# Narrow products among dense blocks, a second z block moved behind the Gram products, and fill products in four waits of TensorE

## What is computed

```python
h = rms_norm(x, pre_mix_norm)
p_r, p_k, p_v, p_c, z_rwkv, z_conv = split(h @ w_in)
# RWKV-7, per head, token after token
def step(S, inp):
    r_t, w_t, k_t, v_t, a_t, b_t = inp
    sa = einsum('bhvk,bhk->bhv', S, a_t)
    S = S * w_t + sa * b_t + v_t * k_t
    return S, einsum('bhvk,bhk->bhv', S, r_t)
# convolution branch: 31 causal taps per channel, then layer norm and silu
c = silu(layer_norm(conv31(u * sigmoid(gate)) + dw_b))
merged = sigmoid(z_rwkv) * (y @ w_rwkv_out) + sigmoid(z_conv) * (c @ w_conv_out)
x = x + rms_norm(merged @ w_out)
x = x + rms_norm((silu(h @ w_gate) * (h @ w_up)) @ w_down)   # h = rms_norm(x, ...)
```

## Time and profile before

| | |
|---|---|
| runs, three | median 1368.31 us, 1367.41 to 1369.19 |
| the profiled execution | 1369.3 us, its span 1367.6 us |
| busy: TensorE | 1321.0 us, 97% of the span |
| busy: VectorE, ScalarE, GpSimd | 995.3, 774.4, 115.8 us |
| mean granted clock of TensorE | 0.988 |
| chain of work that ended last | TensorE 89%, VectorE 7%, issue 2%, ScalarE 2%, DMA 1% |

### The profile page before, as it was taken

The page is one execution under the profiler, slowest core; times in us unless marked ns, Lnnn a source line. Parts: engine busy times, 40 slices in busy tenths (PEclk is TensorE's granted clock), DMA queues, the critical chain, the costliest instruction groups (busy, mean ns, idle before and its releaser), DMA issues.

```text
span 1367.6 us, 30059 instructions
## 1 busy us (share of the span) xinstructions
PE 1321.0 (97%) x12384; PEld 1260.9 (92%) x12384; DVE 995.3 (73%) x1636; ACT 774.4 (57%) x1353; POOL 115.8 (8%) x151
## 2 busy tenths in 40 slices
PE   7999999999999999999997999999999998999998
PEld 6998979889989999989996899999999888999986
DVE  5769998969876665585898867887565666887754
ACT  5596775559455444464669755444455465644443
POOL 3000000000002110000103002221000100122100
PEclk9999999989999999999999999999999999999999
DMA  7634611222545555545572354556563621555561
GB/s 242 205 122 148 194 64 34 86 72 94 193 147 185 182 186 175 187 142 181 177 227 84 103 183 161 182 185 199 173 196 133 224 93 63 185 185 184 176 210 61
DMA packets 197811, 212.70 MB, mean 156 GB/s; under 512 B 8973, under 2 KB 186925, under 8 KB 197565
## 3 DMA queue, kind: packets, MB, share of 16 engines
q1 hardware_dynamic: 195132, 201.46, 45.9%
q0 software_dynamic: 2464, 9.52, 2.4%
q10 hardware_dynamic: 96, 0.02, 0.0%
HBM read 209.33 MB, written 1.65 MB: 154 GB/s over the span
## 4 chain that ended last, share of the span: by engine, by line
PE 89%; DVE 7%; issue 2%; ACT 2%; DMA 1%; SPq 0%; DVEq 0%; ACTq 0%
PE pb L473 21%; PE pb L475 21%; PE pb L474 21%; PE pb L2428 2%; PE pb L2762 1%; PE pb L2763 1%; PE pb L2764 1%; DVE pj L1690 1%; PE pb L2253 1%; PE pb L2264 1%; DVE w_lo L517 1%; PE pb L2697 1%; PE pb L2372 1%; PE pb L2373 1%; PE pb L2374 1%
## 5 line engine op out<-in xcount | busy, mean ns | idle before, releaser
L517 DVE TENSOR_TENSOR w_lo<-raw,w_hi 128x1024 fp32r<-128x1024 f32 (+2 forms) x384 | 466.1, 1217 | 137.6 <-ACT w_hi L511 136.8
L511 ACT ACTIVATE w_hi<-raw 128x1024 fp32r<-128x1024 f32 (+2 forms) x384 | 396.5, 1041 | 280.9 <-PE pb L475 219.5
L473 PE MATMUL pb<-x_hi,w_hi 128*128 128x256 f32 x1848 | 526.0, 285 | 3.1 <-DVE w_lo L517 2.8
L474 PE MATMUL pb<-x_lo,w_hi 128*128 128x256 f32 x1848 | 523.1, 283 | 0.0
L475 PE MATMUL pb<-x_hi,w_lo 128*128 128x256 f32 x1848 | 523.1, 283 | 0.0
L473 PEld LDWEIGHTS pb<-x_hi,w_hi 128*128 128x128 f32 x1848 | 355.0, 192 | 6.0 <-DVE w_lo L517 3.9
L474 PEld LDWEIGHTS pb<-x_lo,w_hi 128*128 128x128 f32 x1848 | 355.0, 192 | 0.2
L475 PEld LDWEIGHTS pb<-x_hi,w_lo 128*128 128x128 f32 x1848 | 354.9, 192 | 0.0
L766 POOL TENSOR_TENSOR sub<-sub,rstd 128x256 f32<-128x256 f32 x66 | 71.8, 1102 | 568.9 <-ACT sub L1159 568.9
L473 PE MATMUL pb<-act_hi,w_hi 128*128 128x256 f32 x392 | 110.9, 283 | 0.0
L475 PE MATMUL pb<-act_hi,w_lo 128*128 128x256 f32 x392 | 110.9, 283 | 0.0
(11 more groups left out here) (369 smaller groups left out, 2273.3 us busy)
## 6 DMA issues: line engine op xcount, KB each, us to landing
raw<-in_ffn_w_up_dram SPq DMA_DIRECT2D x55, 1024.0 KB, 5.1
raw<-in_w_in_dram SPq DMA_DIRECT2D x28, 1024.0 KB, 5.2
raw<-in_ssd_w_in_dram SPq DMA_DIRECT2D x20, 1024.0 KB, 5.3
raw<-in_ffn_w_down_dram SPq DMA_DIRECT2D x16, 1024.0 KB, 5.0
raw<-in_fox_w_in_dram SPq DMA_DIRECT2D x16, 1024.0 KB, 5.8
raw<-in_ffn_w_down_dram SPq DMA_DIRECT2D x16, 896.0 KB, 5.0
raw<-in_ffn_w_gate_dram SPq DMA_DIRECT2D x11, 1024.0 KB, 5.2
raw<-in_ssd_w_out_dram SPq DMA_DIRECT2D x8, 1024.0 KB, 5.9
```

The source lines that it names most:

```text
L473: pe.matmul(o, w_hi[m][:, k, :], hi[:, k0 + k, :], start=first and k == 0, stop=False)
L474: pe.matmul(o, w_hi[m][:, k, :], lo[:, k0 + k, :], start=False, stop=False)
L511: act.activation(piece(ly, u, w_hi[m], nk, m), raw_piece(ly, u, s, nk, m), ACT.Copy).then_inc(sem("w_hi_ready"), 1)
L517: dve.tensor_tensor(piece(ly, u, w_lo[m], nk, m), raw_piece(ly, u, s, nk, m), piece(ly, u, w_hi[m], nk, m).bitcast(F32), ALU.subtract).the ...
```

## The change

The code of the change does five things.

1. **Start.** Eight products of a 128x128 fp32 matrix with itself (`keep_busy`; nothing reads the result) are written behind the first transposes, ahead of layer rk.
2. **Triangle.** The second part of the triangle products is no longer a run behind block 3 of ug: eight of its products follow each k step inside the block, through a new hook `between`. The first part stays where it was.
3. **Inverse and z.** The first z block is taken out of chunk 0 and stands ahead of the chunks, with eight of the second group's 64 inverse products behind each of its k steps. In chunks 0 to 3, which hold two z blocks, the second goes behind the Gram products (`Z_FRONT`). Its evacuation on VectorE moves behind the mask and one tap, ahead of the state sum; its `w_hi` on ACT moves behind `v_rows`. The wait for z evacuations is split: the x products wait for all the blocks before them, the state products for the front ones.
4. **Chunk 4.** Seven fill products ahead of the wait for the copies of u, that is ahead of the state products.
5. **Squares.** Ten fill products behind each of the two `post_squares`, ahead of up0 and ssd_z.

Hunk 473 is in `pe_layer`, 1048 on ScalarE, 1728 on VectorE, those from 2264 on TensorE:

```diff
+        FIRST_SINGLE = Z_CHUNK.index(1)
+        Z_FRONT = [1 if n == 2 else n for n in Z_CHUNK]
...
@@ -473,6 +476,11 @@
                         mm = pe.matmul(o, w_lo[m][:, k, :], hi[:, k0 + k, :], start=False, stop=final and k == nk - 1)
+                        if between and k < nk - 1:
+                            between(u, m, k)
                     mm.then_inc(sem("block_done"), 1)
+                    if between:
+                        between(u, m, nk - 1)
...
@@ -1048,8 +1059,7 @@
-                for j in range(BANKS + Z_FIRST[c], min(BANKS + Z_FIRST[c + 1], len(L["z"]) * M_PER_UNIT)):
-                    z_head(j)
+                z_heads(Z_FIRST[c], Z_FIRST[c] + Z_FRONT[c])
...
                 if c + 1 < NCHUNK:
                     v_rows(c + 1)
+                z_heads(Z_FIRST[c] + Z_FRONT[c], Z_FIRST[c + 1])
...
@@ -1728,7 +1739,7 @@
-                    if i < Z_CHUNK[c]:
+                    if i < Z_FRONT[c]:
                         z_evac(Z_FIRST[c] + i, Z_FIRST[c] + i + 1)
...
                     mask_products(c + 1)
+                taps = DVE_EARLY + sum(DVE_TAPS[:c])
+                if Z_FRONT[c] < Z_CHUNK[c]:
+                    conv_taps(taps, taps + 1)
+                    taps += 1
+                    z_evac(Z_FIRST[c] + Z_FRONT[c], Z_FIRST[c + 1])
+                if c + 1 < NCHUNK:
                     state_sum(c)
-                conv_taps(DVE_EARLY + sum(DVE_TAPS[:c]), DVE_EARLY + sum(DVE_TAPS[:c + 1]))
+                conv_taps(taps, DVE_EARLY + sum(DVE_TAPS[:c + 1]))
...
@@ -2264,6 +2281,11 @@
+            def keep_busy(o, n):
+                for _ in range(n):
+                    mm(o, ident[:, :], ident[:, :], start=True, stop=True, skip_group_check=True)
...
             turn(pb[1][:, 0:P], par_tok[:, 0, :]).then_inc(sem("par_turned"), 1)
+            keep_busy(pb[2][:, 0:P], 8)
...
+            def lower_between(u, m, k):
+                if M_PER_UNIT * u + m == LAB_BLOCK + 1:
+                    lower_pairs(1, 4 * k, 4 * k + 4)
+            pe_layer(pe, L["ug"], x_hi, x_lo, "x_lo_ready", X_BASE[0], lower_products, between=lower_between)
...
+            inverse_turns(0, 0, INV_GROUP)
+            pe.wait_ge(sem("conv_ready"), PE_TILES)
+            z_blocks(Z_EARLY, Z_EARLY + Z_FRONT[0], between=lambda k: inverse_turns(1, INV_GROUP // KC * k, INV_GROUP // KC * (k + 1)))
             pe.wait_ge(sem("inverse_rows"), CHUNK // INV_GROUP)
...
                 if c:
+                    z_out(Z_FIRST[c])
                     pe.wait_ge(sem("u_rows_v"), c)
...
-                if c + 1 < NCHUNK:
-                    z_blocks(Z_FIRST[c], Z_FIRST[c + 1], c)
+                if c and c + 1 < NCHUNK:
+                    z_blocks(Z_FIRST[c], Z_FIRST[c] + Z_FRONT[c], c)
...
                     chunk_products(c + 1)
+                    z_blocks(Z_FIRST[c] + Z_FRONT[c], Z_FIRST[c + 1], c)
...
+                if c == FIRST_SINGLE:
+                    keep_busy(pb[5][:, T:T + P], 7)
                 pe.wait_ge(sem("u_rows_v"), c + 1)
...
-                    z_out(Z_FIRST[c + 1])
+                    z_out(Z_FIRST[c] + Z_FRONT[c])
...
             post_squares(0)
+            keep_busy(pb[6][:, 0:P], 10)
             pe_layer(pe, L["up0"], x_hi, x_lo, "x_lo_ready", X_BASE[1], spread=lambda: norm_sums(1))
             pe_layer(pe, L["down0"], act_hi, act_lo, "act_lo_ready", 0)
             post_squares(1)
+            keep_busy(pb[6][:, 0:P], 10)
```

More of the change, by code:

```diff
@@ L1041, in conv_head, with z_heads @@
                 act.activation(y_hi[:, k, :], slot(GATE)[:, k, :], ACT.Copy).then_inc(sem("x_hi_ready"), 1)
+            def z_heads(first, last):
+                for j in range(BANKS + first, min(BANKS + last, len(L["z"]) * M_PER_UNIT)):
+                    z_head(j)
             for c in range(NCHUNK):
@@ L2341, in _, with lower_pairs @@
             pe_layer(pe, L["v"], x_hi, x_lo, "x_lo_ready", X_BASE[0], v_products)
-            def lower_products(u, m):
-                part = M_PER_UNIT * u + m - LAB_BLOCK
-                if part not in (0, 1):
-                    return
-                if part == 0:
-                    pe.wait_ge(sem("dve_stages"), PAIRS_MADE)
-                    pe.wait_ge(sem("bonus_ready"), 1)
-                for y in range(4 * KC):
+            def lower_pairs(part, first, last):
+                for y in range(first, last):
                     k, c = y % KC, 4 * part + y // KC
```

28 lines of the change are left out of this document (19 added, 9 removed).

## The result

| | before | after |
|---|---|---|
| median of 7 runs | 1367.41 us (1366.67 to 1369.19) | 1371.75 us (1370.47 to 1374.32) |
| profiled execution, span | 1369.3, 1367.6 us | 1372.23, 1370.5 us |
| mean granted clock of the runs | 0.989 (35 later runs) | 0.992 |

The ratio is 1.0026, interval 1.0017 to 1.0036: slower by 4.3 us, where 6 us less were forecast; the time lies above the range.

What follows compares the result with a forecast made beforehand. The prediction took TensorE's own work plus what slows it as the bound. Its terms, -1.15 + 0.9 - 1.6 - 2.9 - 1.2 = -5.95 us off the median 1368.31, gave 1362.4 us, range 1358.8 to 1367.0.

Steps and rivals of the forecast that it cites:

- Bound and views: Whole kernel: TensorE's work plus what slows it, read from its waits, half-clock stretches and instruction sequences.
- ssd_z, "nothing to gain": Fills ahead of ssd_z: the clock already stood at 1.00 there, so no gain was counted.
- Part 1: Start: eight fills hold the clock, norm sum 1.15 us earlier, POOL late next; bounds 0 and 1.15.
- Part 2: Triangle among dense products: stop of 1.54 us goes, switches cost 0.35 a pair; net loss 0.9 us.
- Part 3: Inverse products, z blocks and chunk 4: DVE bounds chunk 1; together 4.5 us gained at the sums of chunk 5.
- The 1.6 us at the state products of chunk 4: Chunk 4: state products start at 269.4, not 270.99, 1.6 us gained; the fills cost 0.8 of it.
- The 2.9 behind chunk 4: From chunk 4's state products to the sums of chunk 5: full clock instead of 0.50, 2.9 us gained.
- Part 4: Ten fills behind the squares: 13 dense products in up0 at 0.12 instead of 0.213, 1.2 us gained.
- A: Switches between narrow and dense products are hidden: triangle gains 1.9 instead of losing 0.9; 1359.6 us, chance 0.15.
- B: In one of the two interleaved blocks the clock falls or the stop stays: 1364.1 to 1365.8 us, chance 0.20.
- C: Clock falls in both interleaved blocks and stays at 0.50 in chunk 0: slower, 1374.8 us, chance 0.07.
- D: Fills fail: clock falls at the start, in chunk 4 and in up0 as before; 1367.6 us, chance 0.10.

Runs made afterwards that it cites:

- g1: Kernel before with one more memset (0.96 us) on POOL ahead of the four transfers of the substitution's input: 1372.13 us, ratio 1.0019.
- g4: Kernel before with the z and inverse change in chunk 0 alone, chunks 1 to 3 in old order, no fills: 1372.08 us, ratio 1.0025.
- g2: Kernel before with the z and inverse change, second z block's evacuation directly behind the mask, triangle in one run, no fills: 1366.60 us, ratio 0.9981.
- e3: Kernel before with only the z and inverse change, evacuation behind the tap, triangle in one run, no fills: 1365.48 us, ratio 0.9983.
- e4: Kernel before with only the triangle's second part among the dense products of block 3, no fills: 1371.14 us, ratio 1.0022.
- h1: Changed kernel with POOL's memsets ahead of the wait for the first transfer, so the substitution's transfers go out earlier: 1368.04 us, ratio 1.0004.
- e1: Changed kernel with the triangle's second part back in one run behind block 3 of ug: 1367.88 us, ratio 1.0000.
- i2: Changed kernel with the substitution's transfers issued earlier and the evacuation directly behind the mask: 1364.45 us, ratio 0.9982.
- g3: Changed kernel with the triangle in one run and without chunk 4's fills, evacuation still behind the tap: 1366.33 us, ratio 0.9978.
- e2: Kernel before with the four sets of fill products and nothing else: 1368.52 us, ratio 1.0000.
- i3: Kernel before with the fills at the start and behind both squares only, none in chunk 4: 1368.34 us, ratio 1.0013.

## Why the prediction was wrong, point by point

- **Bound and views.** Right: TensorE's work plus what slows it. Wrong in use: one profile's list of half-clock stretches was taken as the kernel's. ssd_z, "nothing to gain", fell in 3 of 7 profiles without fills, and chunks 1 to 3 of the old order, clean in the earlier trace rows, fell in 4 of 6.
- **Part 1, start, -1.15.** Measured -1.17, POOL next in line (the wait of L2257 for it is 0.79). The row of the changed kernel, TensorE at the norm sum:

```profile
23.88 0.67 PE L2257 MATMUL pb<-sub,ones 128*128 128x256 f32 x2 [0.79 <-POOL sub L744]
```

  But four of the seven profiles without these fills had the sum 0.4 to 1.1 us earlier too (g1, g4, g2, e3; 0.45 us earlier in the mean of the seven), so the term was worth 0.7 on average.
- **Part 2, triangle, +0.9: the step that failed.** On TensorE the block and the triangle cost 0.25 us more in e4, not 0.9, because the switch was cheaper than the 0.35 of the earlier trace rows: groups 0.77 us apart, of which 0.36 are three dense products and 0.14 the 16 records, leave 0.27. That POOL's issue moved by 0.89 in e4 is luck; it came from the evacuation that now stands behind the whole block. The stop went away in e4 and shrank to 0.81 in the changed kernel:

```profile
127.11 0.29 PE L2372 MATMUL pb<-pj 64*32 64x32 f32 x16
...
127.89 0.24 PE L2372 MATMUL pb<-pj 64*32 64x32 f32 x3
128.95 0.29 PE L2372 MATMUL pb<-pj 64*32 64x32 f32 x13 [0.81 <-issue]
```

  The error is the sentence behind it: what stands behind this block would "move by the same 0.9 us, and DVE, with no wait worth naming until the inverses, keeps them so". It named VectorE's step and left out what follows from it, POOL's transfers, and the weights' transfer that SyncE issues beside them. 0.8 us late there became 2.64 on VectorE. Worth 2.6 to 3.9 us of the total by e4, g1, h1 and e1, medians or ratios. That is the loss, but not the missing gain: with it repaired (h1, 1.0004) the kernel is level with the one before, and with the evacuation ahead of the tap too (i2, 0.9982) it is 2.5 us faster by the ratio, of 6 forecast.
- **Part 3.** The block among inverse products took 0.907 us a group, 7.3 for the whole (forecast 7.5), at full clock:

```profile
206.53 0.43 PE L2474 MATMUL pb<-ident,sub 32*32 32x32 f32 x16
206.89 0.38 PE L2402 MATMUL pb<-x_hi,w_hi 128*128 128x256 f32 x1
...
207.44 0.43 PE L2474 MATMUL pb<-ident,sub 32*32 32x32 f32 x16
```

  VectorE as the bound of chunk 1, and the waits behind it (copies, decay, mask, tap, evacuation: 5.4 forecast, 218.05 to 223.65 = 5.6), were right; the start of this list was put at 215.2 and came at 218.0, through part 2. With the triangle in one run and the tap ahead (e1, e3, g3) the first product of chunk 1 came at 221.31 to 221.85, 220.6 forecast. What I priced at nothing was the wait itself: the clock fell in all four profiles in which TensorE stood 1.6 us or more at the x products, and with the evacuation directly behind the mask the wait is 0 to 0.73 us and it fell in none of six. The 1.6 us at the state products of chunk 4 didn't come: they started at 277.12 (270.99 before), and the fills ended 0.7 us after the copies of u, as the forecast had it (0.8). The 2.9 behind chunk 4 was exact where the fills stood.
- **Part 4, up0, -1.2.** Measured: +4.15 before it, +2.93 behind it. The dense products there stand 0.12 us apart, by the timeline:

```profile
403.97 0.28 PE L425 MATMUL pb<-x_hi,w_lo 128*128 128x256 f32 x1
404.09 0.28 PE L426 MATMUL pb<-x_lo,w_hi 128*128 128x256 f32 x1
```

- **Rivals.** A: switches aren't hidden (0.27), no. B: in the changed kernel neither interleaved block fell, the clock fell behind a wait for VectorE; right behind the inverse block it fell in e1 and g4, so B isn't empty. C gave the sign and even near the number (1374.8) by a mechanism that didn't happen: it needed TensorE late (at the state products of chunk 0 it was 0.78 late, not 7), and what was late was VectorE, by 2.8. D: the fills held the clock, and the total came out as if they hadn't, e2 and i3. The Trainium skill ("TensorE: Matmul & The Clock Gate", Why this matters for your kernels) warns only of longer gaps; the table of places disagrees: behind the wait of chunk 4, 1.0 to 2.65 us in the ten profiles without its fills, the clock fell in 9 of 10.
